# A state-space layer and its projection in one block of queues, and a last projection begun inside banded attention

## The chip, the cores and the metric

The kernel runs on one core of a Trainium2 chip. Its engines run their own queues of instructions in order and meet through semaphores: TensorE (PE) multiplies, VectorE (DVE), ScalarE (ACT) and GpSimd (POOL) do the elementwise work, and SyncE (SP) issues nearly all transfers. The metric is the device time of one execution, in microseconds (us).

## The reference

Two blocks of two layers each act on 1024 tokens of 1024 features, in float32. The first block has a recurrent layer and multi-head latent attention. The second block has a layer in which differential attention and a state-space scan stand side by side, and then banded ("sliding window") attention. Both layers of the second block end in an output projection whose result is added to the residual:

```python
def ssd_scan(xh, dt, A, bm, cm):            # chunks of 128 tokens, 16 heads of 64, 2 groups, state 128
    cs = jnp.cumsum(dA, axis=-1)
    lmat = jnp.exp(segsum(dA))              # decays inside a chunk
    cb = jnp.einsum('bclgn,bcsgn->bcgls', cc, bc)
    y_diag = jnp.einsum('bcgjls,bcsgjp->bclgjp', cb[:, :, :, None] * lmat, xdt)
    states = jnp.einsum('bclgn,bcgjl,bclgjp->bcgjpn', bc, decay_states, xdt)
    # the state is carried from chunk to chunk
    y_off = jnp.einsum('bclgn,bcgjpn,bcgjl->bclgjp', cc, prev, jnp.exp(cs))
    return y_diag + y_off
```

Its output is gated, normed per group, joined to that of differential attention and projected. Banded attention has 16 heads of 64 over 2 key heads, a window of 128 tokens, and a projection of its own.

## The kernel before

**Number format.** Products that must be near float32 are made of three passes of rounded float32: each weight tile (128 output features, 8 blocks of 128 x 128) is split into a high part by ScalarE (`split_hi`, L156) and a rest by VectorE (`split_lo`, L162), and so are the operands `xh` and `xl`. `three_passes` (L167 to L169) issues three matmuls of 512 columns. Weight tiles stream from memory through two slots. `load_ahead` (L147) asks for the tile after next as soon as its slot has been split.

**The state-space stage.** `ssd` (L1947) runs two blocks of queues. A block ends with all engines meeting. In the first, `conv_tiles` makes 12 tiles of input for the scan, and `step_sizes_and_z` makes the step sizes and 8 gate tiles (z). All go to memory. The second is `ssd_chunks` (L2183). It goes over 8 chunks b of 128 tokens:

- PE: `front` turns x and B of a chunk to tokens (L2290 to L2298); the gate is turned (L2346), carried products (L2317), states (L2358), the diagonal product (L2367, L2370), the output is turned back (L2306).
- ACT: tanh of the gate (L2430), `decays(b + 1)` in two passes over 2048 columns (L2398, L2400), squares (L2443), output copy `yt` (L2421), root (L2448), and `by_token` (L2406, L2410).
- DVE: masking (L2543), sums and products of the output, the state (L2568), `differences(b + 1)` (L2492), and the residual.
- POOL: x times step sizes and decays (L2471, L2476, L2482).

Into the loop is woven the part of the output projection that takes the output of differential attention (`project`, 8 tiles of weights, each in two halves of 512 tokens). One bank of PSUM, `pu`, holds the sum of a half tile until VectorE has added it to the residual (`added`, L2514); PE doesn't begin the next half before. In chunk b tile b - 1 is projected, and the 8th follows behind the loop. Its operands are y tiles that are loaded from memory during chunks 0 and 1 through three buffers and split.

**The projections.** `project_halves` (L349) makes 16 half tiles. It loads y in halves (L410), splits them (L533 or L535 on ACT, L618 or L621 on DVE), runs tiles 0 and 1 together operand by operand, then the others, adds each to the residual (L715), and norms the result for the next stage. The projection of the scan's output is a block of its own behind `ssd_chunks`, with a clearing of semaphores between.

**Banded attention.** `window_attention` (L2602) goes over 8 pairs of heads with 8 blocks n of 128 queries each. In every block PE turns the probabilities (L2712), multiplies them with the values (L2729) and makes the scores two blocks on; DVE takes the maximum (L2834) and norms (L2851), ACT takes exponents (L2747). Weight tiles of the next pair are multiplied between these in all pairs but the last. y of a pair is written to memory at its end (L2659). The last projection is again a block of its own behind it.

The order inside a chunk is written out by hand. On ACT it was, and on DVE:

```python
# ACT                                       # DVE
act.activation(tz, pz, ACT.Tanh, ...)       differences(b + 1)
if b: split_hi(act, k, tile(b))             if b: split_lo(dve, k, tile(b))
if b < last: decays(b + 1)                  dve.wait_ge(s["yd"], b + 1)
act.wait_ge(s["yy"], b + 1)   # squares     dve.tensor_tensor(y, px, y, ALU.add)
```

Of the kernel before, what the change touches and what calls it, by code (L numbers as in the profile page):

```python
# [109 lines left out]

class Link:
# [31 lines left out]
def load_ahead(sp, k, j0, h, per, i, further=0):  # L143

    t = Tile(j0, h + 2, per, i)
    sp.wait_ge(k.w_lo[t.slot], t.before)
    sp.dma_start(k.w_raw[:, t.slot, :],  # L147
                 k.stream[bass.ds(k.shift + j0 + 2 + h + per * i + further, 1)].rearrange("a p c -> (a p) c")
                 ).then_inc(k.w_loaded[t.slot], 16)
# [199 lines left out]
def project_halves(k, prefix, y0, kts, after, out=None, gain=None):  # L349
# [10 lines left out]
    k.shift += (stride - 2) * DT  # L360
    ahead = 2 if after != "end" else 0
# [4 lines left out]
    with ExitStack() as c:  # L366
        def sb(name, shape, dt=F32):
            return c.enter_context(nc.sbuf_tensor(prefix + "_" + name, shape, dt))

        raw, sq, tmp = sb("raw", [P, 8, HALF]), sb("sq", [P, 4, HALF]), sb("tmp", [P, 4, HALF])  # L370
        if extra:
            x2h, x2l = (sb(n, [P, extra, S], F32R) for n in ("hi", "lo"))
            w2, w2h, w2l = (sb(n, [P, 2, extra * P], dt) for n, dt in (("w2", F32), ("w2h", F32R), ("w2l", F32R)))
        if double:
            sum2, sq2, gg, st = sb("sum2", [P, S]), sb("sq2", [P, 4, HALF]), sb("gg", [P, DT]), sb("st", [P, 6, QT])
        block = c.enter_context(nc.Block(no_gpsimd_drain=True))
        high = [k.xh[:, d, :] for d in range(DT)] + [x2h[:, d, :] for d in range(extra)]
        low = [k.xl[:, d, :] for d in range(DT)] + [x2l[:, d, :] for d in range(extra)]
        operand_at = [[] for _ in range(tiles)]
        for n in range(kts):  # L380
            operand_at[n * DT // kts].append(kts + n)
        norm_at = {10: (0,), 11: (1, 2), 12: (3, 4), 13: (5, 6), 14: (7,)}

        def tile(q):
            return Tile(j0, q, 2, 0)

        def row(q):
            return row0 + stride * (q % DT) if q < tiles else row0 + stride * DT + q - tiles

        def total(q):  # L390
            return k.aux[:, 0, half(q % 2)]

        def factors(h, n=1):

            return k.aux[:, 1 - h, half(n)]

        def sums(h, n=0):
            at = HALF + 16 * h + HS * n
            return k.acc[:, 1, at:at + HS]

        def resid(q):
            return k.resid[:, q % DT, half(q // DT)]

        @block.sync
        def _(sp):
            def load_y(q):
                h, d = divmod(q, kts)
                if q >= 8:
                    sp.wait_ge(s["lo"], q - 7)
                sp.dma_start(raw[:, q % 8, :], k.y_dram[y0 + d][:, half(h)]).then_inc(s[f"in{q % 8}"], 16)  # L410

            def load_piece(q):
                if q >= 2:
                    sp.wait_ge(s["piece_lo"], q - 1)
                sp.dma_start(w2[:, q % 2, :], k.stream[row(q) + 1][:, 0:extra * P]).then_inc(s[f"piece{q % 2}"], 16)

            def load_weights(q):
                t = tile(q)
                sp.wait_ge(k.w_lo[t.slot], t.before)
                sp.dma_start(k.w_raw[:, t.slot, :], k.stream[row(q)]).then_inc(k.w_loaded[t.slot], 16)  # L420
                if extra and q < tiles:
                    load_piece(q)

            for q in range(8):
                load_y(q)
# [12 lines left out]
            for q in range(6, tiles + 2 * ahead):  # L438
                load_weights(q)
            if after == "end":  # L440
                for h in range(2):
                    for d in range(DT):
                        sp.wait_ge(s["scaled"], DT * h + d + 1)
                        sp.dma_start(out[d][:, half(h)], k.resid[:, d, half(h)]).then_inc(s["stored"], 16)
                sp.wait_ge(s["stored"], 32 * DT)

        @block.tensor
        def _(pe):
            def part(q, kt):
                t = tile(q)  # L450
                if kt < DT:
                    w = slice(kt * P, (kt + 1) * P)
                    w_hi, w_lo = k.w_hi_sb[:, t.slot, w], k.w_lo_sb[:, t.slot, w]
                else:
                    w = slice((kt - DT) * P, (kt - DT + 1) * P)
                    w_hi, w_lo = w2h[:, q % 2, w], w2l[:, q % 2, w]
                x = half(q // DT)
                return three_passes(pe, total(q), w_hi, w_lo, high[kt][:, x], low[kt][:, x], kt == 0, kt == kts - 1)

            def sum_squares(h):  # L460
                pe.wait_ge(s["sum"], 1 + DT + DT * h)
                if double:
                    pe.wait_ge(s["sum2"], 1 + DT + DT * h)
                for n, squares in enumerate((k.stat_sq, sum2) if double else (k.stat_sq,)):
                    for t in range(HS):
                        at = h * HALF + t * P
                        mm = pe.matmul(sums(h, n)[:, t:t + 1], squares[:, at:at + P], k.inv_col[:, 0:1],  # L467
                                       start=True, stop=True)
                mm.then_inc(s["ss"], 1)

            def spread(h):
                pe.wait_ge(s["diag"], (2 if double else 1) * HS * (h + 1))
                if double:
                    pe.matmul(factors(h, 0), k.ones[:, :], sum2[:, half(h)], start=True, stop=True)
                pe.matmul(factors(h), k.ones[:, :], k.stat_diag[:, half(h)], start=True, stop=True  # L475
                          ).then_inc(s["rb"], 1)

            def product(q, kt, n):
                t = tile(q)
                w = slice(kt * P, (kt + 1) * P)  # L480
                return three_passes(pe, bank(k.acc[:, t.slot, :], n), k.w_hi_sb[:, t.slot, w],
                                    k.w_lo_sb[:, t.slot, w], bank(k.xh[:, kt, :], n), bank(k.xl[:, kt, :], n),
                                    kt == 0, kt == DT - 1)

            for q in range(2):
# [9 lines left out]
            for q in range(2, tiles):  # L495
                wait_tile(pe, k, tile(q))
                if extra:
                    pe.wait_ge(s["piece_lo"], q + 1)
                for kt in range(kts):
                    if q == DT:  # L500
                        pe.wait_ge(s["lo"], kts + kt + 1)
                    mm = part(q, kt)
                mm.then_inc(k.tile_done[tile(q).slot], 1)
                if q == 9:
                    sum_squares(0)
                if q == 10:
                    spread(0)
            if after == "end":
                sum_squares(1)
                spread(1)  # L510
                return
            for q in (tiles, tiles + 1):
                wait_tile(pe, k, tile(q))
                for kt in range(DT):
                    pe.wait_ge(s["nlo"], kt + 1)
                    product(q, kt, 0)
                    if q == tiles and kt == 3:
                        sum_squares(1)
            spread(1)
            for kt in range(DT):  # L520
                pe.wait_ge(s["nlo"], DT + kt + 1)
                for q in (tiles, tiles + 1):
                    mm = product(q, kt, 1)
                    if kt == DT - 1:
                        mm.then_inc(k.tile_done[tile(q).slot], 1)

        @block.scalar
        def _(act):
            def operand(q):
                h, d = divmod(q, kts)  # L530
                act.wait_ge(s[f"in{q % 8}"], 16 * (q // 8) + 16)
# [1508 lines left out]
def step_sizes_and_z(k, c, tab):  # L2040
# [139 lines left out]
    return block  # L2180


def ssd_chunks(k, tab):  # L2183

# [902 lines left out]
```

## Time and profile before

| | |
|---|---|
| median of 3 runs | 2817.12 us (2814.34 to 2817.89) |
| the profiled execution | 2814.39 us, its span 2812.6 us |
| mean granted clock of TensorE | 0.961 of full speed |
| busy share of the span | PE 91%, DVE 57%, ACT 43%, POOL 7% |
| instructions | 32482 |

How to read the profile: "idle before" or the bracket behind a row is the time that the engine stood still before it, and what released it. PEclk 1.00 is the full clock of 2.4 GHz, 0.50 is 1.2 GHz. A row with x8 merges eight instructions, and its time is that of all.

### The profile page before, as it was taken

What the parts mean: (1) busy time and instruction counts of PE and PEld (TensorE: products, weight loads), DVE (VectorE), ACT (ScalarE), POOL (GpSimd) and SP (SyncE); (2) the same over time, 40 slices, a digit from 0 to 9 for tenths busy, and PEclk for the clock granted to TensorE, in tenths of its full rate; (3) what the DMA queues carried; (4) which work ended last, traced back from release to release, by engine and by line L of the source; (5) the groups of instructions that cost most, each with busy time, mean ns of one, the idle gap of its engine ahead of it and who ended that gap; (6) DMA issues with size and microseconds to landing.
All of it is one profiled execution on the core that took longest, in us unless ns stands there. A gap on an engine that the chain in (4) does not pass through costs nothing. (4 is left out here: it accounts for less than half of the span.)

```text
span 2812.6 us, 32482 instructions
## 1 busy us (share of the span) xinstructions
PE 2560.6 (91%) x12125; PEld 2092.3 (74%) x12125; DVE 1597.2 (57%) x2881; ACT 1217.1 (43%) x2061; POOL 202.7 (7%) x114
## 2 busy tenths in 40 slices
PE   5999598988999889899999997999599898999978
PEld 4777487867777767788888885788477686888856
DVE  6655465335555546666666664542566454666654
ACT  3555333224444433455555553431445334454432
POOL 0000021000000034000000000000232120000012
PEclk9999799999999989999999997999799998999998
DMA  2211431222121142111110100223543420111033
GB/s 103 73 68 55 147 95 58 67 90 75 53 90 51 55 135 68 38 38 38 38 36 32 38 31 15 89 97 101 181 146 113 132 85 27 40 36 45 31 120 113
DMA packets 89974, 207.05 MB, mean 74 GB/s; under 512 B 7152, under 2 KB 39792, under 8 KB 88816
## 3 DMA queue, kind: packets, MB, share of 16 engines
q1 hardware_dynamic: 89840, 205.25, 22.1%
q8 instruction: 86, 1.41, 0.2%
q14 instruction: 48, 0.39, 0.0%
HBM read 164.26 MB, written 40.96 MB: 73 GB/s over the span
## 5 line engine op out<-in xcount | busy, mean ns | idle before, releaser
L167 PE MATMUL acc<-operand_hi,w_hi 128*128 128x512 f32 x1830 | 742.5, 406 | 49.9 <-DVE w_lo L162 12.2
L169 PE MATMUL acc<-operand_hi,w_lo 128*128 128x512 f32 x1830 | 722.6, 395 | 0.0
L168 PE MATMUL acc<-operand_lo,w_hi 128*128 128x512 f32 x1830 | 721.2, 394 | 0.0
L167 PEld LDWEIGHTS acc<-operand_hi,w_hi 128*128 128x128 f32 x1830 | 348.8, 191 | 132.9 <-issue 37.8
L169 PEld LDWEIGHTS acc<-operand_hi,w_lo 128*128 128x128 f32 x1830 | 348.0, 190 | 76.7
L168 PEld LDWEIGHTS acc<-operand_lo,w_hi 128*128 128x128 f32 x1830 | 349.1, 191 | 69.7 <-issue 2.6
L156 ACT ACTIVATE w_hi<-w_raw 128x1024 fp32r<-128x1024 f32 (+1 forms) x209 | 202.7, 970 | 360.0 <-PE aux L169 184.3
L162 DVE TENSOR_TENSOR w_lo<-w_raw,w_hi 128x1024 fp32r<-128x1024 f32 (+1 forms) x209 | 233.1, 1115 | 217.4 <-ACT w_hi L156 217.1
L167 PE MATMUL aux<-operand_hi,w_hi 128*128 128x512 f32 x650 | 265.0, 408 | 70.3 <-DVE w_lo L162 36.5
L169 PE MATMUL aux<-operand_hi,w_lo 128*128 128x512 f32 x650 | 257.9, 397 | 0.0
L168 PE MATMUL aux<-operand_lo,w_hi 128*128 128x512 f32 x650 | 257.8, 397 | 0.0
L167 PEld LDWEIGHTS aux<-operand_hi,w_hi 128*128 128x128 f32 x650 | 125.4, 193 | 106.7 <-issue 73.8
L168 PEld LDWEIGHTS aux<-operand_lo,w_hi 128*128 128x128 f32 x650 | 125.5, 193 | 26.6 <-issue 1.5
L169 PEld LDWEIGHTS aux<-operand_hi,w_lo 128*128 128x128 f32 x650 | 124.8, 192 | 27.0
L1858 DVE TENSOR_REDUCE att<-aux 128x1 f32<-128x256 f32 (+3 forms) x128 | 104.8, 819 | 50.4 <-PE aux L1626 50.1
L715 DVE TENSOR_TENSOR resid<-aux,resid 128x512 f32<-128x512 f32 x64 | 44.1, 689 | 115.9 <-PE aux L169 115.7
L1809 ACT ACTIVATE da_pth<-acc 128x512 f32<-128x512 f32 (+1 forms) x96 | 47.2, 525 | 143.4 <-PE acc L1640 143.1
L596 POOL MEMSET stat_sq<- 128x1024 f32 x4 | 3.8, 951 | 1200.3 <-POOLq L1159 469.1
L2796 ACT ACTIVATE sw_pth<-aux 128x512 f32<-128x512 f32 x64 | 38.2, 597 | 115.2 <-PE aux L2712 115.2
L1388 ACT ACTIVATE mlah_pth<-acc 128x512 f32<-128x512 f32 (+1 forms) x96 | 48.6, 525 | 88.0 <-PE acc L1276 87.9
L1416 DVE TENSOR_REDUCE att<-aux 128x1 f32<-128x256 f32 (+3 forms) x64 | 52.5, 820 | 58.5 <-PE aux L1256 57.7
L2747 ACT ACTIVATE sw_probs<-aux,sw_st 128x256 f32<-128x256 f32 x128 | 59.5, 470 | 53.5 <-DVE sw_st L2839 52.0
(401 smaller groups left out, 4288.4 us busy)
## 6 DMA issues: line engine op xcount, KB each, us to landing
w_raw<-in_stream SPq DMA_DIRECT2D x209, 512.0 KB, 3.7
ssd_e<-cs_scratch SPq DMA_DIRECT2D x8, 1024.0 KB, 6.9
g_scratch<-conv_y SPq DMA_DIRECT2D x12, 512.0 KB, 2.9
ssd_xbc<-g_scratch SPq DMA_DIRECT2D x8, 768.0 KB, 4.7
y_scratch<-rnn_y SPq DMA_DIRECT2D x10, 512.0 KB, 3.1
out_a_raw<-y_scratch SPq DMA_DIRECT2D x20, 256.0 KB, 5.5
resid<-in_x SPq DMA_DIRECT2D x8, 512.0 KB, 7.6
g_scratch<-mlai_g SPq DMA_DIRECT2D x8, 512.0 KB, 2.9
```

The lines of the kernel that those rows point to most:

```text
L156: act.activation(k.w_hi_sb[:, t.slot, 0:width], k.w_raw[:, t.slot, 0:width], ACT.Copy).then_inc(k.w_hi[t.slot], 1)
L162: dve.tensor_tensor(k.w_lo_sb[:, t.slot, 0:width], k.w_raw[:, t.slot, 0:width], as_f32(k.w_hi_sb[:, t.slot, 0:width]), ALU.subtract).then_ ...
L167: pe.matmul(out, w_hi, x_hi, start=first, stop=False)
L168: pe.matmul(out, w_hi, x_lo, start=False, stop=False)
L169: return pe.matmul(out, w_lo, x_hi, start=False, stop=last)
L715: dve.tensor_tensor(resid(q), total(q), resid(q), ALU.add).then_inc(k.acc_free[t.slot], 1)
L1388: act.activation(pth[t // 2 % 2][:, at:at + w, (t % 2) * P:(t % 2 + 1) * P], slots[at // 4][:, 0:w * P].rearrange("p (n q) -> p n q", q=P) ...
L1416: dve.reduce_max(st[:, 0, :], k.aux[:, t % 2, 0:att_keys(t)], AX.X).then_inc(s["top"], 1)
L1809: act.activation(pth[:, at:at + w, (t % 2) * P:(t % 2 + 1) * P], slots[at // 4][:, 0:w * P].rearrange("p (n q) -> p n q", q=P), ACT.Copy). ...
L1858: dve.reduce_max(st[:, 0, :], k.aux[:, m, 0:att_keys(t)], AX.X).then_inc(s["top"], 1)
L2747: act.activation(probs[:, n % 2, e, :], scores[n % 2][:, e * QG:(e + 1) * QG], ACT.Exp, scale=0.125, bias=t[:, 2, e:e + 1], accum_out=t[:, ...
L2796: act.activation(pth[:, n % 2, :], turned, ACT.Copy).then_inc(s["pth"], 1)
```

## The change

Stages give their programs as objects, and a new `together` runs several of them one after the other in one block of queues. The whole state-space layer (input tiles, step sizes and gate, chunks, second projection) is now one such block, and so are banded attention and the last projection.

In the state-space layer the buffers of all parts lie in one place. Loads of x for chunks 0 and 1, of the cumulative sums of chunk 0 and of four y tiles are issued during the z tiles, as are the differences and decays of chunk 0. The y operands go through five buffers. Chunk 0 is written out of the loop, with another order of its products. Output tile b is projected in chunk b. In the loop ACT now splits tile b + 1 behind the decays. The halves of y for the second projection are loaded before the last chunk has ended.

In banded attention the last pair now carries tiles 0 and 1 of the last projection over the first 512 tokens (`Begun`), operand by operand; its sums lie in a slot of `acc`. The last projection has four y buffers in place of eight, and loads the second halves only.

The diff, cut to its core (lines of which only the indentation changes aren't shown; `Chunks` holds buffers and the bodies of loads, differences and decays, unchanged but for the y buffers):

```diff
+def together(k, *stages):
+    with k.nc.Block(no_gpsimd_drain=True) as block:
+        @block.sync
+        def _(sp):
+            for stage in stages:
+                stage.sp(sp)
...
+class Begun:
+    def load(self, sp, d):
+        n = len(self.raw)
+        if d >= n:
+            sp.wait_ge(self.s["lo"], d - n + 1)
+        sp.dma_start(self.raw[d % n], self.k.y_dram[self.y0 + d][:, half(0)]).then_inc(self.s[f"in{d % n}"], 16)
...
+    def part(self, pe, d):
+        k = self.k
+        w = slice(d * P, (d + 1) * P)
+        pe.wait_ge(self.s["lo"], d + 1)
+        for q in range(2):
+            t = self.tile(q)
+            if d == 0:
+                wait_tile(pe, k, t)
+            mm = three_passes(pe, self.totals[q], k.w_hi_sb[:, t.slot, w], k.w_lo_sb[:, t.slot, w],
+                              k.xh[:, d, half(0)], k.xl[:, d, half(0)], d == 0, d == DT - 1)
+            if d == DT - 1:
+                mm.then_inc(k.tile_done[t.slot], 1)
...
 # project_halves, SP, when tiles 0 and 1 are begun already
+        else:
+            for q in range(kts, kts + n_raw):
+                load_y(q)
+            for q in (2, 3):
+                load_weights(q)
+            for q in range(kts + n_raw, 2 * kts):
+                load_y(q)
+                load_weights(q - kts - n_raw + 4)
+            for q in range(kts - n_raw + 4, tiles + 2 * ahead):
+                load_weights(q)
...
 # step_sizes_and_z
+        for h in range(2):
+            tile(iters - 1, h)
+            if h == 0 and "end" in between:
+                between["end"]()
...
         def store_cs():
             sp.wait_ge(s["cst"], 1)
             sp.dma_start(k.cs_dram.rearrange("c (h l) -> (c h) l", l=P), cst).then_inc(s["stored"], 16)
+            sp.wait_ge(s["stored"], 16)
+            m.load_c(sp, 0)
+            for d in range(4):
+                m.load_y(sp, d)
...
+        rounds(act, tile, {0: exp_steps, 3: exp_sums, "end": lambda: m.decays(act, 0)})
...
 # ssd_chunks, SP
+        m.load_z(sp, 0)
+        for d in (4, 5, 6):
+            m.load_y(sp, d)
+        sp.wait_ge(s["ylo"], 4)
+        m.load_c(sp, 1)
...
+            if b == last:
+                sp.wait_ge(s["yd"], last)
+                sp.wait_ge(s["stored"], 16 * (QT // 2))
+                for q in range(4):
+                    m.load_half(sp, q)
...
 # ssd_chunks, PE
+        front(0)
+        diagonal(0)
+        turn_gate(0)
+        states(0)
+        project(0, 0, early)
+        front(1)
+        project(0, 0, late)
+        project(0, 1, early)
+        project(0, 1, late)
+        for b in range(1, QT):
+            turn_gate(b)
+            carried(b, 0)
+            project(b, 0, early)
+            carried(b, 1)
+            if b < last:
+                states(b)
+            diagonal(b)
+            project(b, 0, late)
             pe.wait_ge(s["zs"], b + 1)
             turn_output(b - 1)
-            project(b - 1, 1, early)
+            project(b, 1, early)
             if b < last:
                 front(b + 1)
-            project(b - 1, 1, late)
-        project(last, 0, range(DT))
+            project(b, 1, late)
         pe.wait_ge(s["yt"], last)
         turn_output(last)
-        project(last, 1, range(DT))
...
 # ssd_chunks, ACT
+        by_token(0)
+        for d in range(4):
+            operand(d)
+        gate(0)
+        operand(4)
+        operand(5)
+        m.decays(act, 1)
+        operand(6)
+        operand(7)
+        by_token(1)
+        squares(0)
+        root(0)
+        split_hi(act, k, tile(1))
+        for b in range(1, QT):
+            gate(b)
+            if b < last:
+                m.decays(act, b + 1)
+            split_hi(act, k, tile(b + 1))
+            squares(b)
+            output(b - 1)
+            root(b)
...
 # ssd_chunks, DVE
+        causal(0)
+        masked(0)
+        for d in range(4):
+            operand(d)
+        summed(0)
+        state(0)
+        m.differences(dve, 1)
+        operand(4)
+        operand(5)
+        gated(0)
+        times_gate(0)
+        operand(6)
+        operand(7)
+        causal(1)
+        variance(0)
+        added(0, 0)
+        split_lo(dve, k, tile(1))
+        for b in range(1, QT):
+            masked(b)
+            added(b - 1, 1)
+            carried(b, 0)
+            gated(b)
+            carried(b, 1)
+            norm(b - 1)
+            if b < last:
+                state(b)
+                m.differences(dve, b + 1)
+            split_lo(dve, k, tile(b + 1))
+            summed(b)
+            times_gate(b)
+            added(b, 0)
+            variance(b)
...
 # window_attention: SP, PE, ACT, DVE in the last pair
+            if last:
+                for d in range(SW_PAIRS - 1):
+                    sp.wait_ge(s["stored"], 16 * d + 16)
+                    begun.load(sp, d)
...
+                elif n:
+                    begun.part(pe, n - 1)
...
+                if last:
+                    if n == 0:
+                        act.wait_ge(k.tile_done[g_tile(i, par).slot], g_tile(i, par).before + 1)
+                        split_hi(act, k, begun.tile(1))
+                    if n < SW_PAIRS - 1:
+                        begun.high(act, n)
+                    if n == 6:
+                        act.wait_ge(s["y"], ready)
+                        begun.high(act, SW_PAIRS - 1, y[:, 0:HALF])
...
+                if last:
+                    if n == 0:
+                        split_lo(dve, k, begun.tile(1))
+                    if n < SW_PAIRS - 1:
+                        begun.low(dve, n)
+                    if n == 6:
+                        begun.low(dve, SW_PAIRS - 1, y[:, 0:HALF])
```

## Rows read from the trace of the kernel before

**Rows 1.** Stretches: busy time of each engine, granted clock, DMA share, GB/s

```profile
1975.33:2048.95 73.62, 44.59 (x222) 35.57 (x223) 40.38 (x38) 35.85 (x39) 18.11 (x8) 0.72 0.59 207
2048.95:2191.65 142.70, 138.01 (x788) 111.52 (x785) 96.66 (x124) 65.71 (x79) 37.92 (x15) 1.00 0.35 115
2191.65:2213.80 22.15, 12.21 (x56) 9.81 (x57) 6.03 (x7) 4.97 (x6) 0.95 (x1) 0.85 0.32 100
2660.43:2717.03 56.60, 33.67 (x162) 26.25 (x160) 28.97 (x88) 23.39 (x59) 1.66 (x2) 0.88 0.31 112
```

**Rows 2.** Timeline of PE in chunk 5: start, us, instruction

```profile
2121.85 1.03 PE L2346 MATMUL acc<-ident,ssd_zc 128*128 128x128 f32 x8
...
2137.36 0.39 PE L167 MATMUL aux<-operand_hi,w_hi 128*128 128x512 f32 x1
...
2138.04 1.03 PE L2306 MATMUL acc<-ident,ssd_yy 128*128 128x128 f32 x8
2138.99 0.50 PE L167 MATMUL aux<-operand_hi,w_hi 128*128 128x512 f32 x1
...
2146.15 1.03 PE L2346 MATMUL acc<-ident,ssd_zc 128*128 128x128 f32 x8
```

**Rows 3.** Timeline of DVE in chunk 5

```profile
2131.94 2.28 DVE L2492 TENSOR_TENSOR ssd_e<-ssd_e,ssd_tab 128x2048 f32<-128x2048 f32 x1
2134.14 1.22 DVE L162 TENSOR_TENSOR w_lo<-w_raw,w_hi 128x1024 fp32r<-128x1024 f32 x1
2135.45 1.23 DVE L2580 TENSOR_TENSOR ssd_yy<-acc,ssd_yy 128x1024 f32<-128x1024 f32 x1
2136.70 1.23 DVE L2585 SCALAR_TENSOR_TENSOR ssd_yy<-ssd_yy,stat_diag 128x1024 f32<-128x1024 f32 x1
2138.24 0.69 DVE L2514 TENSOR_TENSOR resid<-aux,resid 128x512 f32<-128x512 f32 x1 [0.31 <-PE aux L169]
```

**Rows 4.** Timeline of ACT in chunks 5 and 6

```profile
2134.26 1.92 ACT L2398 ACTIVATE ssd_e<-ssd_e 128x2048 f32<-128x2048 f32 x1 [9.36 <-DVE ssd_e L2492]
2136.20 1.92 ACT L2400 ACTIVATE ssd_e<-ssd_e 128x2048 f32<-128x2048 f32 x1
...
2142.91 1.02 ACT L2406 ACTIVATE ssd_xs<-acc 128x1024 f32<-128x1024 f32 x1 [1.15 <-PE acc L2290]
...
2148.14 1.05 ACT L156 ACTIVATE w_hi<-w_raw 128x1024 fp32r<-128x1024 f32 x1
```

**Rows 5.** Stretches behind two pauses of PE, columns as in rows 1

```profile
2027.08:2033.00 5.92, 5.92 (x10) 2.82 (x10) 3.77 (x10) 0.00 (x0) 1.10 (x1) 0.50 0.01 3
2213.80:2217.50 3.70, 3.69 (x9) 2.93 (x10) 3.44 (x6) 3.45 (x6) 0.00 (x0) 0.50 1.03 404
```

**Rows 6.** The masked product: ns min/median/max, first and last start

```profile
L2543 DVE TENSOR_TENSOR ssd_e<-ssd_e,ssd_cbm x8: 2277/3958/3959, 1993.6 to 2168.4; 128x2048 f32<-128x2048 f32 x8
```

**Rows 7.** Splitting one y operand, as in rows 6

```profile
L2505 DVE TENSOR_TENSOR operand_lo<-ssd_hd,operand_hi x3: 1216/1226/1808, 1995.8 to 2019.6; 128x1024 fp32r<-128x1024 f32 x3
```

**Rows 8.** Loads of the cumulative sums of a chunk (`ssd_e`), from issue

```profile
DMA to landing us min/median/max: 6.7/6.9/11.8
```

**Rows 9.** First operand of the second projection on ACT, timeline

```profile
2209.57 0.72 ACT L535 ACTIVATE operand_hi<-out_ssd_raw,vec 128x512 fp32r<-128x512 f32 x1 [9.45 <-DMA out_ssd_raw<-y_scratch]
```

**Rows 10.** Timeline of DVE, last pair: y of two successive blocks

```profile
2677.94 0.60 DVE L2900 SCALAR_TENSOR_TENSOR stat_sq<-aux,sw_g 64x128 f32<-64x128 f32 x2
...
2681.76 0.60 DVE L2900 SCALAR_TENSOR_TENSOR stat_sq<-aux,sw_g 64x128 f32<-64x128 f32 x2
```

**Rows 11.** Splitting a half operand of the last projection

```profile
L618 DVE TENSOR_TENSOR operand_lo<-out_sw_raw,operand_hi x16: 691/693/1787, 2699.4 to 2746.9; 128x512 fp32r<-128x512 f32 x16
```

**Rows 12.** Timeline of SP between banded attention and last projection

```profile
2692.71 0.35 SPq L2659 DMA_DIRECT2D y_scratch<-stat_sq  x1
2695.80 3.89 SPq L410 DMA_DIRECT2D out_sw_raw<-y_scratch  x8
```

**Rows 13.** Loads of weight tiles (`w_raw`) from 2690 to 2720, from issue

```profile
DMA to landing us min/median/max: 3.6/6.2/7.0
```

More of the change, by code:

```diff
@@ L365, in project_halves @@
                        "chain diag rb gg scaled nhi nlo ws stored")
[L366 to L422, printed above, removed]
@@ new lines, in project_halves, with tile, row, total @@
+    low = [k.xl[:, d, :] for d in range(DT)] + [x2l[:, d, :] for d in range(extra)]
+    operand_at = [[] for _ in range(tiles)]
+    for n in range(kts):
+        operand_at[n * DT // kts].append(kts + n)
+    norm_at = {10: (0,), 11: (1, 2), 12: (3, 4), 13: (5, 6), 14: (7,)}
+    def tile(q):
+        return Tile(j0, q, 2, 0)
+    def row(q):
+        return row0 + stride * (q % DT) if q < tiles else row0 + stride * DT + q - tiles
+    def total(q):
+        if begun is not None and q < 2:
+            return begun.totals[q]
+        return k.aux[:, 0, half(q % 2)]
@@ L439, in _ @@
                 load_weights(q)
[L440 to L479, printed above, removed]
-                w = slice(kt * P, (kt + 1) * P)
-                return three_passes(pe, bank(k.acc[:, t.slot, :], n), k.w_hi_sb[:, t.slot, w],
-                                    k.w_lo_sb[:, t.slot, w], bank(k.xh[:, kt, :], n), bank(k.xl[:, kt, :], n),
-                                    kt == 0, kt == DT - 1)
@@ L494, in _ @@
                         mm.then_inc(k.tile_done[tile(q).slot], 1)
[L495 to L507, printed above, removed]
@@ new lines, in _ @@
+        for q in range(2, tiles):
+            wait_tile(pe, k, tile(q))
+            if extra:
+                pe.wait_ge(s["piece_lo"], q + 1)
+            for kt in range(kts):
+                if q == DT:
+                    pe.wait_ge(s["lo"], kts - q0 + kt + 1)
+                mm = part(q, kt)
+            mm.then_inc(k.tile_done[tile(q).slot], 1)
+            if q == 9:
+                sum_squares(0)
+            if q == 10:
+                spread(0)
+        if after == "end":
+            sum_squares(1)
+            spread(1)
+            return
@@ new lines, in _ @@
+        for q in range(tiles):
+            for n in operand_at[q]:
+                operand(n)
+            t = tile(q)
+            act.wait_ge(k.tile_done[t.slot], t.before + 1)
+            if q + 2 < tiles + ahead:
+                if after == "latent" and q + 2 >= tiles:
+                    act.wait_ge(s["ws"], q + 3 - tiles)
+                split_hi(act, k, tile(q + 2))
+                if extra and q + 2 < tiles:
+                    piece(q + 2)
+            act.wait_ge(k.acc_free[t.slot], t.before + 1)
+            if q >= 4:
+                act.wait_ge(s["sum"], q - 2)
+            act.activation(sq[:, q % 4, :], resid(q), ACT.Square).then_inc(s["one"], 1)
+            if double:
+                if q >= 4:
+                    act.wait_ge(s["sum2"], q - 2)
+                act.activation(sq2[:, q % 4, :], resid(q), ACT.Square,
+                               scale=k.vec[:, VEC["final1"] + q % DT:VEC["final1"] + q % DT + 1]
+                               ).then_inc(s["one2"], 1)
+            if q == 9:
+                roots(0)
+            if after != "end":
+                for d in norm_at.get(q, ()):
+                    norm(0, d)
@@ new lines, in _ @@
+        roots(1)
+        if after != "end":
+            for d in range(DT):
+                norm(1, d)
+    @block.gpsimd
+    def _(pool):
+        for sem, value in own.get("free", ()):
+            pool.wait_ge(sem, value)
+        pool.memset(k.stat_sq[:, :], 0.0).then_inc(s["sum"], 1)
+        if double:
+            pool.memset(sum2[:, :], 0.0).then_inc(s["sum2"], 1)
+        for q in range(tiles):
+            at = half(q // DT)
+            pool.wait_ge(s["one"], q + 1)
+            pool.wait_ge(s["sum"], q + 1)
+            pool.tensor_tensor(k.stat_sq[:, at], k.stat_sq[:, at], sq[:, q % 4, :], ALU.add).then_inc(s["sum"], 1)
+            if double:
+                pool.wait_ge(s["one2"], q + 1)
+                pool.wait_ge(s["sum2"], q + 1)
+                pool.tensor_tensor(sum2[:, at], sum2[:, at], sq2[:, q % 4, :], ALU.add).then_inc(s["sum2"], 1)
+        pool.wait_ge(s["sum"], 1 + tiles)
+        if double:
+            pool.wait_ge(s["sum2"], 1 + tiles)
```

1733 lines of the change are left out of this document (886 added, 847 removed).

## The prediction

> **What bounds the kernel now.** I read the page first, then the busy time of each engine in stretches around the places that the diff touches [rows 1], then, inside these, the order of instructions engine by engine. In the steady part of the state-space chunks (2048.95 to 2191.65) TensorE is busy 138.0 of 142.7 us at full clock: it is the bound there, and an edit pays only if it takes idle time from it. The idle time sits in three places. From the end of the last z tile (1975.33) to the gate transposes of chunk 2 (2048.95) 73.6 us pass with 44.6 busy, at a mean clock of 0.72. From the end of the sixth output tile (2191.65) to the first matmul of the second projection (2213.80) 22.15 us pass, of which one output tile (24 matmuls for each half) and a transpose are the work. And from the start of the last pair of banded attention to the third projection tile of the last stage (2660.43 to 2717.03) 56.6 us pass with 33.7 busy. The diff aims at exactly these three. What it does besides to the steady chunks has to be looked for with equal care, since whatever it costs is paid six times.
>
> Unit prices. Three matmuls start within 0.68 us of the next three (2137.36 to 2138.04), so half an output tile (24 matmuls) is 5.45 us at full clock [rows 2]. A copy of 1024 columns on ScalarE is 1.0 us, a weight split 1.05 us there and 1.22 us on VectorE [rows 3, 4]. One chunk is 24.3 us (gate of chunk 5 at 2121.85, of chunk 6 at 2146.15) [rows 2]; five of them in the 142.7 us leave 21.2 for chunk 7 up to 2191.65, as it has no state and no next front [rows 1].
>
> **Part 1, the steady chunks.** Matmul work stays what it was; tile b moves into chunk b. The queues of ScalarE and VectorE keep their order in the loop except for one step. Before, ScalarE ran gate(b), the weight split, then decays(b+1). Now it is gate(b), decays(b+1), the split. VectorE has not changed its own order: differences(b+1), then its half of the split (`w_lo`), which waits for ScalarE's half, then the sum of the chunk, times the gate, and the addition into the residual that frees the one bank `pu` which TensorE's second half tile needs.
>
> Before, ScalarE's split came 12 us ahead, straight behind the gate (as at 2148.14), and VectorE's followed its differences without a wait (2134.14) [rows 3, 4]. After, ScalarE can start the decays only when the differences are done (2134.26). They are two passes of 1.92, done at 2138.1; its split takes until 2139.2, and only then VectorE's split runs, to 2140.4. The sum that started at 2135.45 starts at 2140.45, 5.0 late; the product follows to 2142.9, the addition (0.69) to 2143.65. TensorE wants that bank right behind the transpose of 2138.04, at 2138.99 [rows 2 to 4]. So it stands idle for 4.8 us in each of the six chunks that have decays (b = 1 to 6). Nothing behind it can fill in, because front(b+1) is queued behind this half tile, and by_token, causal and masked of the next chunk wait for front. No slack takes it back either: from front on, the next chunk is the old chain.
>
> The clock adds to that. After the pauses of before the granted clock is 0.50 for the 5.92 us from 2027.08 and for the 3.70 us from 2213.80, with TensorE busy all the time [rows 5]; that is the 1.2 GHz level, and half of each stretch, 3.0 and 1.9 us, is lost. A pause of 4.8 us is shorter than those two (6.1 and 9.1). I take 2.0 for each, with 0 and 3.0 as ends. So the swap costs 6.8 us in a chunk, 40.8 in all (ends 28.8 and 46.8). The Trainium skill ("TensorE: Matmul & The Clock Gate", HAM oscillation) says that a wait repeated in every iteration pays the fall and the recovery of the clock each time; by that rule the price is 6.8 in a chunk and 40.8 in all, and without it 4.8 and 28.8, which would turn the sum from slower to level (rival (a)). The rows after single pauses agree with it.
>
> **Part 2, the opening.** Removed: the end of a block, and the loads of chunk 0 behind it. The loads of x, of the cumulative sums and of four y tiles, and the decays of chunk 0, go under the z tiles; the z tiles leave ScalarE and VectorE idle most of the time, so I cost them at nothing (if a weight tile comes late behind those 3 MB, some us at most). Counting from 1975.33: front(0) and causal(0) end at 2.3. masked(0) takes 4.0 beside GpSimd's products (2.28 alone, 3.96 in most chunks [rows 6]), so the diagonal starts at 6.2 and ends at about 13, with part of it at half clock. Gate, states, half of the half tile and front(1) follow to 21. They are not what sets the end. That is VectorE and ScalarE: four operands at 1.22 [rows 7] end at 11 to 12; only then the sums of chunk 1 may be loaded, since they go where y tiles lie. They land 6.9 us later, up to 11.8 [rows 8]: 20. Differences 2.3: 22.3. Decays 3.85: 26.2. Operands 6 and 7 copied: 28.2. xs and B of chunk 1 copied: 29.6. Squares, two passes of 0.7 as for 512 columns [rows 9]: 31. Variance and addition: 32.1. Then TensorE runs the second half of tile 0, 5.45 plus 2.5 for a low clock after ten nearly idle us: 40. The gate of chunk 1 starts at 40 (ends 36 and 44), with output tile 0 done.
>
> **Part 3, the seam to the second projection.** Removed: a block end, a barrier, and an output tile behind the last chunk. The y halves are loaded before the chunk ends. Left behind the last half tile are: transpose 0.95, copy to `yt` 1.0, two operands 0.7 each, split 1.05, VectorE's split 1.22, and some 0.1 for each hand-over: 6.0. It isn't shorter because ScalarE has output(7) ahead of the operands, and the first matmul waits for the split of tile 1.
>
> Sum of parts 1 to 3: opening 40, chunk 1 30.4 (24.3 less 0.7, plus 6.8; [rows 1] leave 4.7 us of idle time in six chunks, which is TensorE waiting for the addition that VectorE runs behind masked(b), and in chunk 1 that comes early), chunks 2 to 6 5 x 31.1 = 155.5, chunk 7 21.2, seam 6.0: 253.1. Before it was 238.5. So this stage gets 14.6 us slower: 26.2 are gained at both ends, and 40.8 are given back in the middle.
>
> **Part 4, the last pair.** VectorE's chain sets its pace: 3.82 us a block, from 2677.94 to 2681.76 [rows 10], with max, exponent, norm and y in series. The edit puts a half operand (0.69 [rows 11]) into each of seven blocks and an eighth into block 6, and a split (1.22) into block 0. The pair gets 6.8 us longer. TensorE's six extra matmuls in a block (1.4 us) fit beside it. The first two tiles are then done with the pair. But weights of the third are asked for by SyncE behind the wait for the last store of y: before, store at 2692.71, next issue at 2695.80, eight issues 3.89 [rows 12]. After: store 2699.5, landed 2702.5, four y issues to 2704.5, weights landed 3.6 to 6.2 later [rows 13], 2708.1 to 2710.7, two splits: 2710.4 to 2713.1, and 2.0 lost to the clock after this pause. That stands against 2717.03 [rows 1]. I take 3.5 us gained, with 7 gained and 1 lost as ends.
>
> Sum: 14.6 - 3.5 = 11.1 us slower. The profiled execution took 2814.39 us around its span of 2812.6, which gives 2825.5. It lies 2.7 below the median of the three runs (2817.12), so the median comes to 2828.2.
>
> **Rivals.** (a) The pause comes, but the clock stays up, as it does over the gaps of 0.8 us in the steady chunks [rows 1]: part 1 costs 28.8, and the sum is 14.6 - 12.0 - 3.5 = -0.9, 2816.2. For it: a pause of 4.8 us is shorter than any that I have shown. Against: the clock fell in both that I show.
> (b) The split doesn't hold TensorE: faster. If VectorE's sum were not late, or the addition had slack, the gain at both ends would stand: 14.6 - 40.8 - 3.5 = -29.7, 2787.4. Against: TensorE restarted at 2138.99, only 0.06 behind the end of the addition (2138.24 + 0.69), so 5 us of delay on VectorE have no cover. It decides at the price of one pause: the gains are 26.2 + 3.5 = 29.7, so below 5.0 us in a chunk the change gains, above it loses.
> (c) Opening and last pair go worse: sums landed after 11.8, the last y tile loaded late, and the weights of the last stage at their worst. About 5 more: 2833.
>
> **Numbers.** Forecast 0.60, its own range 2820 to 2840. (a) 0.17, (b) 0.10, (c) 0.13. 0.2% of 2817.1 is 5.6 us, about what a measurement of this kernel tells from no change: 2811.5 to 2822.8. Slower: nearly all of the forecast and (c), hence 0.68 after the lower edge of the forecast. Same: most of (a) and that edge, 0.19. Faster: (b) and the gaining edge of (a), 0.13. The range reaches into (a), up to the worse end of the clock and opening, and leaves out (b): 2812 to 2841.
>
> **What would show it.** Each step has its place in the profile after: VectorE's `w_lo` in chunks 1 to 6 waits 4.9 us for ScalarE's `w_hi`, where it did not wait before; TensorE waits 4.8 us for the addition into `resid` once a chunk, with a clock of 0.50 behind it; gates of chunks 2 to 6 lie 31 us apart; the gate of chunk 1 starts 40 us after the last z tile; 6 us lie between the last half tile and the projection; the last pair takes 39 us in place of 32, and about 10 us of pause follow it. I am wrong if the gates stay 24 to 25 us apart, or if the clock stays at 1.00 behind pauses of 4.8 us.

## The result, and the profile after

The changed kernel takes 2821.7 us (median of 14 runs, 2817.5 to 2828.1) against 2817.05 us before (14 runs). The ratio is 1.0020, 95% interval 1.0012 to 1.0029: 4.65 us slower. The forecast was 2828 with its own range of 2820 to 2840 (the range stated in the end is 2812 to 2841). The profiled execution took 2818.81 us, its span 2817.0, so here too the profile lies 2.9 us below the median.

The stretches of the state-space stage, of the last pair, and behind it, in the changed kernel. As in [rows 1], the columns are the stretch and its length, the busy us (and number of instructions) of TensorE, of its weight loads, of VectorE, ScalarE and GpSimd, then the granted clock, the DMA share and GB/s:

```profile
1972.16:2012.49 40.33, 31.34 (x137) 25.10 (x135) 28.39 (x20) 20.86 (x24) 12.55 (x5) 0.79 0.51 176
2012.49:2194.82 182.33, 152.56 (x805) 122.03 (x804) 99.09 (x121) 72.64 (x84) 39.91 (x16) 0.92 0.33 110
2194.82:2221.60 26.78, 21.31 (x125) 17.56 (x124) 16.23 (x29) 10.36 (x16) 0.98 (x1) 0.99 0.29 89
2666.62:2718.25 51.63, 31.62 (x162) 25.38 (x161) 28.50 (x88) 22.72 (x59) 1.67 (x2) 0.88 0.31 103
2718.25:2722.00 3.75, 3.75 (x9) 2.98 (x10) 3.67 (x4) 1.83 (x3) 1.86 (x2) 0.50 0.62 168
```

The first three lines are the stage from the last z tile to the first matmul of the second projection: 249.44 us, where [rows 1] had 238.47. It is 11.0 us longer. The loss is in the second line: six chunks in 182.3 us, at a mean clock of 0.92, where chunks of [rows 2] take 24.3 each. The fourth line answers to the last of [rows 1], 51.63 for 56.60. The fifth is the low clock behind the pause of the last pair, of which half, 1.9 us, is lost. Behind the same point of before there was none (1.00 from 2717.03 to 2720.80); there the low clock came at the first tile, behind a pause of 10.64 us.

VectorE in chunk 5 of the changed kernel (the order is that of [rows 3]):

```profile
2143.87 2.28 DVE L2127 TENSOR_TENSOR ssd_e<-ssd_e,ssd_tab 128x2048 f32<-128x2048 f32 x1
2151.03 1.23 DVE L192 TENSOR_TENSOR w_lo<-w_raw,w_hi 128x1024 fp32r<-128x1024 f32 x1 [4.87 <-ACT w_hi L186]
2152.17 1.22 DVE L2717 TENSOR_TENSOR ssd_work<-acc,ssd_work 128x1024 f32<-128x1024 f32 x1
2153.42 1.22 DVE L2726 SCALAR_TENSOR_TENSOR ssd_work<-ssd_work,stat_diag 128x1024 f32<-128x1024 f32 x1
2154.56 0.68 DVE L2666 TENSOR_TENSOR resid<-aux,resid 128x512 f32<-128x512 f32 x1
```

ScalarE in the same chunk, answering to [rows 4], and TensorE from the gate of chunk 5 to that of chunk 6:

```profile
2146.19 1.91 ACT L2134 ACTIVATE ssd_e<-ssd_e 128x2048 f32<-128x2048 f32 x1 [10.34 <-DVE ssd_e L2127]
2148.14 1.92 ACT L2136 ACTIVATE ssd_e<-ssd_e 128x2048 f32<-128x2048 f32 x1
2149.96 1.04 ACT L186 ACTIVATE w_hi<-w_raw 128x1024 fp32r<-128x1024 f32 x1
```

```profile
2133.76 1.03 PE L2493 MATMUL acc<-ident,ssd_zc 128*128 128x128 f32 x8
...
2155.30 0.80 PE L197 MATMUL aux<-operand_hi,w_hi 128*128 128x512 f32 x1 [4.30 <-DVE resid L2666]
...
2164.53 1.03 PE L2493 MATMUL acc<-ident,ssd_zc 128*128 128x128 f32 x8
```

One instruction on ScalarE stands behind two passes, VectorE waits 4.87 us for it, and TensorE waits 4.30 us for the addition, which stands behind the split in VectorE's queue. The six chunks take 29.24, 30.30, 30.90, 30.83, 30.77 and 30.29 us from gate to gate.

### The profile page after: what moved, and what is told of

It reads as the page before. It is cut to its first block and busy times, and to the rows that moved or that the text cites. A ratio compares the mean times of both kernels' runs of the same rounds, so it can differ in the third digit from the quotient of the medians.

```text
span 2817.0 us, 32395 instructions
## 1 busy us (share of the span) xinstructions
PE 2565.9 (91%) x12125; PEld 2096.3 (74%) x12125; DVE 1600.3 (57%) x2881; ACT 1216.3 (43%) x2061; POOL 201.2 (7%) x114
## 3 DMA queue, kind: packets, MB, share of 16 engines
q1 hardware_dynamic: 89696, 204.98, 22.2%
```

## The experiments

"The changed kernel" is the one above. Each ratio is that of a kernel to the kernel before, run on the same chip in the same rounds; differences from the changed kernel are those of the medians. A ratio compares runs of the same rounds, so it need not be the quotient of two medians: for kernel 1 it says 35 us less than before, the medians say 33.

| kernel | median us | ratio, 95% interval |
|---|---|---|
| changed kernel | 2821.7 | 1.0020 (1.0012 to 1.0029) |
| 1 split moved back | 2783.75 | 0.9874 (0.9859 to 0.9889) |
| 2 sum ahead of the split on VectorE | 2782.2 | 0.9877 (0.9861 to 0.9892) |
| 3 pauses filled with idle work | 2808.5 | 0.9964 (0.9950 to 0.9978) |
| 4 split between the decays' passes | 2804.1 | 0.9948 (0.9933 to 0.9962) |
| 5 part 4 undone | 2827.2 | 1.0036 (1.0023 to 1.0048) |
| 6 part 4 alone | 2811.1 | 0.9978 (0.9969 to 0.9987) |
| 7 weights asked for early | 2817.8 | 1.0004 (0.9994 to 1.0013) |
| 8 and split first | 2812.0 | 0.9987 (0.9978 to 0.9996) |
| 9 kernels 1 and 8 together | 2775.4 | 0.9857 (0.9842 to 0.9871) |
| 10 opening filled | 2821.9 | 1.0016 (1.0006 to 1.0025) |
| 11 kernel 9, opening filled and reordered | 2773.1 | 0.9844 (0.9829 to 0.9859) |
| 12 kernel 9, opening filled | 2773.1 | 0.9843 (0.9827 to 0.9858) |

**1. The split moved back.**

```diff
             gate(b)
+            split_hi(act, k, tile(b + 1))
             if b < last:
                 m.decays(act, b + 1)
-            split_hi(act, k, tile(b + 1))
             squares(b)
```

> The changed kernel, with one line of ScalarE moved back: in chunks 1 to 6 it splits tile b + 1 before the decays of chunk b + 1. Theory (the late split stops VectorE, and with it TensorE): VectorE's half of the split no longer waits 4.9 us, TensorE's pause of 4.3 us in each of six chunks is gone and the clock stays at 1.00 there; gates lie 24.3 us apart in place of 29.2 (once) and 30.6 (five times), so 36.5 us less than the changed kernel: 2785 us, 32 less than the kernel before. Rival 1 (only the pause goes, the clock stays as it was): 6 x 4.3 = 25.8 less, 2796 us. Rival 2 (the pause has another cause in the new order, such as the place of tile b in chunk b): nothing changes, 2822 us.

2783.75 us, 38 less than the changed kernel. The six chunks of its trace in one line:

```profile
2017.75:2162.52 144.77, 140.90 (x806) 113.98 (x805) 99.53 (x121) 72.01 (x84) 39.91 (x16) 1.00 0.41 135
```

144.8 us for 182.3, a clock of 1.00 throughout, and no pause over 1.5 us. Both rivals fall. The swap of one instruction was the loss, and the rest of the change is worth 33 us: the stage takes 212.2 us from the last z tile (1977.08) to the second projection (2189.29), 26.3 less than before, and part 4 gives the rest.

**2. The sum goes ahead, the split stays late.**

```diff
                 m.differences(dve, b + 1)
-            split_lo(dve, k, tile(b + 1))
             summed(b)
             times_gate(b)
             added(b, 0)
+            split_lo(dve, k, tile(b + 1))
             variance(b)
```

> The changed kernel with ScalarE's late split left as it is; instead VectorE's half of the split goes behind the addition of the first half tile. Theory (what costs time is that the sum, the product and the addition are queued behind a waiting instruction, not that the split is late): the same 36.5 us less as with the split moved back, 2785 us, with ScalarE's split still at its late place. Rival (the lateness of the weights itself is what counts, since TensorE or the loads of the next tile wait for them): less than half of it is gained, over 2804 us.

2782.2 us, as good as kernel 1. The rival (over 2804 us) falls. One line of ScalarE and two of VectorE in one chunk:

```profile
2101.64 1.04 ACT L186 ACTIVATE w_hi<-w_raw 128x1024 fp32r<-128x1024 f32 x1
```

```profile
2099.06 1.22 DVE L2717 TENSOR_TENSOR ssd_work<-acc,ssd_work 128x1024 f32<-128x1024 f32 x1 [1.22 <-PE acc L2515]
...
2102.71 1.23 DVE L192 TENSOR_TENSOR w_lo<-w_raw,w_hi 128x1024 fp32r<-128x1024 f32 x1 [0.16 <-ACT w_hi L186]
```

The weights are as late as in the changed kernel and nobody is hurt: they are for the next chunk. What cost time is that the sum stood behind an instruction that waited.

**3. The pauses filled.** The 18 matmuls write a bank that nobody reads before it is written again.

```diff
             turn_output(b - 1)
+            if b < last:
+                pe.wait_ge(s["y1"], 2 * b)
+                for _ in range(18):
+                    pe.matmul(po, k.ident_r[:, :], k.mask_r[:, :], start=True, stop=True)
             project(b, 1, early)
```

> The changed kernel with 18 matmuls of 512 columns on constant operands, whose result nobody reads, put behind the output transpose of each chunk from 1 to 6: 18 x 0.227 = 4.1 us of extra work inside the pause of 4.3 us. Theory (each pause also costs some 2.0 us of low clock behind it): the clock stays at 1.00 through the chunks, gates lie 28.6 us apart, and the kernel is 12 us faster than the changed one though it does more work: 2810 us. Rival (the low clock is no consequence of the pause, or costs nothing): 2822 us, or a few us more if the extra matmuls run over the pause.

2808.5 us: 13 us faster with 108 matmuls more. Chunks 2 to 6 of this kernel, then three stretches behind pauses of 4.30 us in the changed kernel:

```profile
2042.34:2185.74 143.40, 138.53 (x762) 111.27 (x761) 83.48 (x101) 60.58 (x70) 37.87 (x15) 1.00 0.33 112
```

```profile
2063.29:2066.70 3.41, 3.41 (x10) 2.67 (x11) 0.17 (x1) 3.11 (x7) 0.00 (x0) 0.64 0.27 83
2093.57:2097.00 3.43, 3.43 (x8) 2.75 (x9) 0.17 (x1) 3.10 (x7) 0.00 (x0) 0.50 0.28 87
2155.30:2158.70 3.40, 3.40 (x8) 2.72 (x9) 0.17 (x1) 3.11 (x7) 0.00 (x0) 0.50 0.29 85
```

28.7 us a chunk at a clock of 1.00, where the changed kernel has 30.6 and falls to 0.50 behind each pause (in three of the six only after the first matmuls, hence 0.64). The wait is still paid; 1.9 us a chunk was the clock.

**4. A shorter delay.**

```diff
         act.activation(ef, ef, ACT.Relu, scale=-1.0).then_inc(self.s["e2"], 1)
+        if between is not None:
+            between()
         act.wait_ge(self.s["e2"], b + 1)
...
             if b < last:
-                m.decays(act, b + 1)
-            split_hi(act, k, tile(b + 1))
+                m.decays(act, b + 1, lambda: split_hi(act, k, tile(b + 1)))
+            else:
+                split_hi(act, k, tile(b + 1))
```

> The changed kernel with ScalarE's split between the two passes of the decays, 1.9 us earlier than in the changed kernel. Theory (what VectorE is late, TensorE waits): the pause in chunks 1 to 6 is 4.3 - 1.9 = 2.4 us, and gates lie 26.7 us apart if the clock stays up behind so short a pause (2798 us, from 2783.75 measured without the pause) or 28.7 if it falls as behind the pauses of 4.3 (2810 us). Rival (the first 2 us of a delay are free and only the rest counts, or the pause comes whole): 2783.75 or 2821.7 us.

2804.1 us. All six pauses are 2.34 or 2.35 us, as forecast: what VectorE is late, TensorE waits. Of the clock neither answer holds, and the total lies between the two (2798 and 2810 us). Four of the six chunks:

```profile
2060.86:2064.30 3.44, 3.44 (x8) 2.79 (x9) 0.17 (x1) 3.10 (x7) 0.00 (x0) 0.51 0.77 287
2089.15:2092.60 3.45, 3.45 (x18) 2.86 (x19) 0.17 (x1) 3.11 (x7) 0.00 (x0) 1.00 0.77 288
2115.93:2119.30 3.37, 3.37 (x17) 2.83 (x18) 0.17 (x1) 3.11 (x7) 0.00 (x0) 1.00 0.72 266
2142.65:2146.10 3.45, 3.45 (x8) 2.78 (x9) 0.17 (x1) 3.10 (x7) 0.00 (x0) 0.51 0.73 264
```

Behind one and the same pause it falls in two of six chunks (28.26 and 28.30 us from gate to gate) and stays up in four (25.73 and three of 26.8).

**5. and 6. Part 4 undone, and alone.** Kernel 5 has banded attention and the last projection of the kernel before, kernel 6 the state-space layer and second projection of it.

> The state-space layer of the changed kernel with banded attention and the last projection of the kernel before, so part 4 of the change alone is undone. Theory (begun tiles are worth 5.0 us up to the third tile and lose 2.2 of it again to the clock behind the pause): this kernel is 2.7 us slower than the changed one, 2824.4 us. Rival 1 (with its end, part 4 is worth nothing): 2821.7 us. Rival 2 (it costs time): 2818 us or less.

> The state-space layer and the second projection of the kernel before, with banded attention and the last projection of the changed one: part 4 of the change alone. Theory (part 4 gains what its stretch shows, 5.0 us up to the third tile, less 2.2 for the clock behind the pause): 2.7 us less than the kernel before, 2814.4 us; if the difference of 5.5 us that undoing it made holds, 2811.6 us. Rival (part 4 is worth nothing by itself): 2817 us.

Undoing part 4 costs 5.5 us (2827.2), having it alone gives 6.0 (2811.1 to 2817.1; interval 3.7 to 8.7). The two agree, so the parts add up. Both say more than the 2.7 us that I read from one profile, which lie outside the interval of kernel 6. From the first matmul of the last pair to the third tile kernel 5 has the same instructions as the kernel before, and its profile shows:

```profile
2668.68:2728.26 59.58, 36.26 (x163) 28.08 (x161) 28.79 (x88) 23.30 (x59) 1.67 (x2) 0.80 0.29 106
```

That is 3.0 us longer than the 56.60 of [rows 1], at a clock of 0.80 for 0.88. So the one profile of before that I subtracted from was a fast one in this stretch, which is enough for the missing 3 us. Why the clock differs between the two executions is not shown. Kernel 5 is the state-space part alone: 1.0036, some 10 us slower, as the stretches say (11.0).

**7. and 8. The weights of the last projection.** Kernel 7 issues the loads of tiles 2 and 3 inside the last pair:

```diff
                     begun.load(sp, d)
+                for q in (2, 3):
+                    begun.load_weights(sp, q)
             sp.wait_ge(s["y"], 2 * QT * (p + 1))
```

Kernel 8 in addition puts the operand of step q behind the split of tile q + 2 on ScalarE and VectorE.

> The changed kernel; SyncE asks for weight tiles 2 and 3 of the last projection during the last pair, before it waits for the last y, and no longer behind it. Theory (the pause of 12.9 us ends with these weights): the pause gets some 4 us shorter, as ScalarE's first operand, which is queued ahead of the split, still waits for a half of y asked for behind the last store (landed 6.1 us after it); the kernel takes 2817.6 us, 4 less than the changed one. Rival (the store and the loads of y set the end of the pause): 2821.7 us.

> The same, and ScalarE and VectorE split tile q + 2 ahead of the operand of step q. Theory: the third tile starts behind one split on ScalarE and one on VectorE, 2.6 us behind the last begun matmul in place of 12.9; 10.2 us less than the changed kernel, and up to 2.2 more if the clock doesn't fall over so short a pause: 2809.3 to 2811.5 us. Rival (operands of the second half are now late and TensorE waits for them at tile 8): 5 us or less are gained, 2816.7 us or more.

SyncE around the last store in the changed kernel (compare [rows 12]), and TensorE's third tile in kernels 7 and 8:

```profile
2704.66 0.35 SPq L2832 DMA_DIRECT2D y_scratch<-stat_sq  x1
2707.28 1.75 SPq L506 DMA_DIRECT2D sw_raw<-y_scratch  x4
2709.08 0.90 SPq L516 DMA_DIRECT2D w_raw<-in_stream  x2
```

```profile
2719.29 0.79 PE L197 MATMUL aux<-operand_hi,w_hi 128*128 128x512 f32 x1 [8.20 <-DVE w_lo L192]
```

```profile
2708.02 0.50 PE L197 MATMUL aux<-operand_hi,w_hi 128*128 128x512 f32 x1 [1.80 <-DVE w_lo L192]
```

The pause goes from 12.87 us to 8.20 and to 1.80. The first step gives 3.9 us, as forecast. The second gives 5.8 more, 9.7 in all, a little under the 10.2 to 12.4 forecast; the rival (5 or less) falls. So the weights asked for behind a store were late, and once they are early, a split behind an operand is. In the trace of kernel 8 the clock stays at 1.00 behind 1.80 us.

**9. Both repairs.**

> The split moved back in the chunks (2783.75 us measured alone, 38 less than the changed kernel) together with the weights asked for and split early in the last projection. Theory (the two pauses have nothing to do with each other): the gains add up, 2783.75 less 10.2 to 12.4, so 2771.3 to 2773.5 us, 44 less than the kernel before. Rival (some of the gain of one is a gain of the other, through the clock or the loads): 2776 us or more.

2775.4 us, 8.4 less than kernel 1, 1.4% less than before. It lies between the two answers. The intervals are some 4 us wide to either side, so it doesn't tell them apart.

**10 to 12. The opening.** Kernel 10 puts 18 such matmuls between `front(0)` and `diagonal(0)`, kernel 12 does so in kernel 9, and kernel 11 also runs operands 4 and 5 ahead of the differences of chunk 1 on VectorE.

> The changed kernel with 18 matmuls of 512 columns on constant operands, whose result nobody reads, in the 4.8 us in which TensorE waits for the masked product of chunk 0. They keep the clock up for the diagonal product, gate and states of chunk 0, which took 14.2 us at half clock. Theory (the sums of chunk 1, asked for 12.4 us behind the last z tile, land some 7 to 8 us later and then bound VectorE's chain, 2 us ahead of where the states let it start): gate 1 comes 40.3 - 2 = 38.3 us behind the last z tile, 2 us less in all, 2819.7 us. Rival 1 (only TensorE's products bound the opening): 6 us less, gate 1 at 34 us, 2815.7 us. Rival 2 (the chain on ScalarE and VectorE is bound by their own work throughout): nothing, 40.3 us.

> The kernel with the split moved back and the weights of the last projection asked for and split early (2775.4 us), together with the filled wait in the opening, and operands 4 and 5 of chunk 0 ahead of the differences of chunk 1 on VectorE. Theory (both shorten VectorE's chain of the opening, down to where the sums land): 2 to 3 us less, 2773 us. Rival (the opening is bound elsewhere, or the load of the eighth operand ends it): 2775 us or more.

> The kernel with the split moved back and the weights of the last projection asked for and split early (2775.4 us, ratio 0.9857), with the filled wait in the opening alone: operands 4 and 5 keep their place on VectorE. Theory (the 3.3 us by which the filled wait shortened the opening in its stretch count in the whole too): gate 1 some 37 us behind the last z tile, 2772 us, ratio 0.9845. Rival (they are taken back by the clock further on, as the filled opening alone suggests, whose total did not move): 2775 us or more.

The changed kernel's first products, then the openings of kernels 10 and 12, each from the last z tile to the gate of chunk 1, with a later stretch of kernel 12:

```profile
1978.51:1992.66 14.15, 14.15 (x60) 12.66 (x61) 7.22 (x5) 2.29 (x3) 1.50 (x1) 0.52 0.71 251
2006.92:2012.49 5.57, 5.57 (x25) 4.57 (x25) 4.41 (x2) 2.41 (x3) 4.15 (x2) 1.00 0.00 0
```

```profile
1975.48:2012.52 37.04, 29.56 (x154) 23.35 (x153) 28.43 (x20) 20.86 (x24) 12.56 (x5) 0.86 0.55 192
```

```profile
1979.75:2020.26 40.51, 32.09 (x154) 25.36 (x153) 29.38 (x20) 20.77 (x24) 12.68 (x5) 0.79 0.53 175
2012.09:2017.40 5.31, 5.31 (x13) 4.14 (x14) 4.46 (x2) 2.10 (x2) 3.96 (x2) 0.50 0.00 0
```

VectorE's differences of chunk 1 in the changed kernel, with the copy of the state ahead of them, and in kernels 10 and 12:

```profile
1993.26 1.23 DVE L2710 COPY ssd_work<-aux 128x1024 f32<-128x1024 f32 x1 [3.37 <-PE aux L2501]
1994.40 2.28 DVE L2127 TENSOR_TENSOR ssd_e<-ssd_e,ssd_tab 128x2048 f32<-128x2048 f32 x1
```

```profile
1994.75 2.29 DVE L2127 TENSOR_TENSOR ssd_e<-ssd_e,ssd_tab 128x2048 f32<-128x2048 f32 x1 [3.51 <-DMA ssd_e<-cs_scratch]
```

```profile
1999.94 2.29 DVE L2139 TENSOR_TENSOR ssd_e<-ssd_e,ssd_tab 128x2048 f32<-128x2048 f32 x1 [4.40 <-DMA ssd_e<-cs_scratch]
```

Counted from the last z tile the differences start at 22.2, 19.3 and 20.2 us, and the gate of chunk 1 at 40.3, 37.0 and 40.5. Unfilled, the differences stand behind the copy that waits for TensorE, which works through the diagonal product, the gate and the states at 0.52. Filled, they wait for the sums. So the theory of kernel 10 names what binds, and its 38.3 us came out as 37.0. It fell short of the 34 us of rival 1.

These 3 us are not safe. TensorE idles later when filled (3.96 and 2.03 us in kernel 10, 4.86 and 2.03 in kernel 12). In kernel 10 the second half of tile 0 then runs at 1.00, as unfilled; in kernel 12 its first 5.3 us run at 0.50, and the opening is as long as unfilled. Kernel 11's is 40.55, with a wait of 8.51 us for operands, so its reordering gains nothing.

The total of kernel 10 shows no gain (2821.9 us), but an interval of 2.7 us to either side doesn't rule out 3. The totals of kernels 11 and 12 are what was forecast, 2773 us, while the openings that were to bring it did not get shorter. So these two hits prove nothing, and 2773 against the 2775.4 of kernel 9 lies within the intervals.

## Why the prediction was right, and where it was off

**Direction and mechanism.** That the change gets slower through the swap on ScalarE is shown by kernels 1 and 2. Rival (b), that the split doesn't hold TensorE, falls with them, rival (a) with the 30.6 us of a chunk and with kernel 3, and rival (c) with the opening's 40.3 us and the 5.0 us gained by the third tile. Its price without the swap, 2787.4 us in rival (b), is what kernel 1 measures within 4 us, and the 26.2 us that both ends were to gain are 26.3 in its trace: the gain is real and was given back in the middle.

**The pause** was put at 4.8 us and is 4.30 in every one of the six. VectorE's wait was put at 4.9 and is 4.87. The pause is shorter than the wait because the addition no longer waits 0.31 for TensorE, and VectorE's operations follow each other more closely than I added up. (Before, ScalarE's split at 2123.84 stood 10.3 us ahead of VectorE's half, not 12; the sum doesn't use this.)

**The clock** was put at 2.0 us for each pause, ends 0 and 3.0. Chunks 2 to 6 take 30.6 us; less 24.3 and 4.3 leaves 2.0, and filling the pauses takes 1.9 of it back. The Trainium skill ("TensorE: Matmul & The Clock Gate", HAM oscillation) says of a loop that waits for loads that it pays the fall and the recovery of the clock in every iteration. Here the wait is for another engine. Behind pauses of 4.30 us the trace agrees in all six chunks; behind those of 2.35 us (kernel 4) in two of six. So a chunk cost 6.3 us and not 6.8, and in chunk 1 5.95 (29.24 less the 23.29 of kernel 1).

**The opening** came to 40.3 us for 40, but by another road, and this step failed: "They are not what sets the end." The diagonal product was to end at about 13 us and ended at 16.3, since it ran at half clock all the way, and gate and states too. The states ended at 20.5, and VectorE could start the differences only behind them, at 22.2 in place of 20. Against that, the second half of tile 0 ran at full clock (5.57 us), where I had added 2.5. The two errors cancel, and that the total of the opening came out right is luck. The sums of chunk 1, which I named as the bound, were only the next one, 2 to 3 us earlier, as the filled openings show.

**Chunk 7 and the seam** (the stretch up to the second projection) are 26.8 us together for 27.2 forecast. In the seam TensorE idles 4.7 us.

**The sum of the stage** is thus 11.0 us longer in place of 14.6: 2.4 less in chunks 2 to 6, 1.2 in chunk 1, 0.4 at the end, 0.3 more in the opening.

**Part 4.** The pair got 5.8 us longer for 6.8 (from its first matmul to the last store 38.0 us for 32.3), the pause behind it was 12.87 us for "about 10 us", the third tile came 5.0 us earlier than before, and the clock took 1.9 of it. What was mis-sized is the term of 3.5 us gained in all: kernels 5 and 6 measure 5.5 and 6.0. Against the profile of kernel 5, with its lower clock in this stretch, the third tile came 7.9 us earlier, which less 1.9 is 6.0.

**The total.** Stage 11.0 and part 4 of -6.0 give +5.0, measured +4.65. So the forecast of +11 was 6.4 us too high, 3.6 of it from the stage and 2 to 2.5 from part 4, each inside its stated ends. The measured difference is less than half of the one forecast, and 2821.7 us lies in what the prediction itself called "same" (2811.5 to 2822.8, chance 0.19) and not in "slower" (0.68): that it is slower at all is told by 14 runs of each, whose interval leaves out 1.

## What to carry to other kernels

When a queue is written out by hand, an instruction may be as late as its own reader allows, but nothing that another engine needs may stand behind its wait. Look at the queue of the waiting engine, not only at who needs the late result. A pause repeated in a loop can cost more than its length, by the clock behind it (here some 2 us behind 4.3 every time, behind 2.35 twice in six), and a gain at the ends of a loop is quickly given back by a few microseconds in each round. Loads that don't depend on a store belong ahead of the wait for it.

## What was not expected of the hardware

Work without use made the kernel faster: 108 matmuls in six pauses took 13 us off. At equal pauses of 2.35 us the granted clock fell in some chunks and not in others of one execution, and in the opening of kernel 12 filling one wait moved the half clock to later products.

Executions of the same instructions differ by more than many edits: the last z tile ended at 1972.16 us in the profile of the changed kernel and at 1979.75 in that of kernel 12, whose edits all come later. So single profiles are compared here stretch by stretch, and a total only by its rounds.
